# Tail steps carried into the next stream, a root on 128x2, norms tile by tile

## What is computed

```python
for i in range(2):
    mod = (cs @ ada_w[i] + ada_b[i])[:, None, :]          # cs = silu(c)
    sh1, sc1, g1, sh2, sc2, g2 = jnp.split(mod, 6, axis=-1)
    h = rms_norm(x, norm1_g[i]) * (1.0 + sc1) + sh1
    mix = dilated_attention(h, ...) if i == 0 else s5_mixer(h, ...)
    x = x + g1 * mix
    h = rms_norm(x, norm2_g[i]) * (1.0 + sc2) + sh2
    x = x + g2 * conv_ffn(h, ...)       # up product, conv, silu(gate) * up, down product
return rms_norm(x, final_norm_g)        # rms_norm: x * rsqrt(mean(x * x) + 1e-6) * g
```

## Times and profile before

| | us |
|---|---|
| median of 3 runs | 3445.22 (3442.17 to 3446.24) |
| profiled execution | 3444.99 |
| its span, first to last instruction | 3443.2 |
| PE busy | 3022.7 (88% of the span) |
| DVE busy | 2394.6 (70%) |
| ACT busy | 1246.4 (36%) |
| POOL busy | 924.3 (27%) |

### The profile page before, as it was taken

The page is one execution under the profiler, slowest core; times in us unless marked ns, Lnnn a source line. Parts: engine busy times, 40 slices in busy tenths (PEclk is TensorE's granted clock), DMA queues, the critical chain, the costliest instruction groups (busy, mean ns, idle before and its releaser), DMA issues.

```text
span 3443.2 us, 60362 instructions
## 1 busy us (share of the span) xinstructions
PE 3022.7 (88%) x22810; PEld 2833.7 (82%) x22810; DVE 2394.6 (70%) x2649; ACT 1246.4 (36%) x1716; POOL 924.3 (27%) x728
## 2 busy tenths in 40 slices
PE   7899999999769998899988576666997998999997
PEld 3499999999769998899987544443996998999997
DVE  7566666666668887878768698999556664456545
ACT  0144444444224443244432222222433553344432
POOL 2101111111571104720049554555312110001111
PEclk9999999999889999999999797887998999999999
DMA  8977777777556877877667322221553554655453
GB/s 284 340 276 254 258 253 254 253 260 268 190 183 246 301 268 294 301 291 279 240 230 273 137 81 90 79 84 41 180 201 117 183 182 146 186 179 183 165 162 110
DMA packets 227200, 714.37 MB, mean 207 GB/s; under 512 B 40928, under 2 KB 45792, under 8 KB 226656
## 3 DMA queue, kind: packets, MB, share of 16 engines
q1 hardware_dynamic: 185184, 666.98, 56.2%
q10 hardware_dynamic: 41856, 45.19, 4.0%
HBM read 689.01 MB, written 23.07 MB: 207 GB/s over the span
## 4 chain that ended last, share of the span: by engine, by line
PE 67%; DVE 12%; POOL 11%; issue 7%; DMA 2%; ACT 1%; ACTq 0%; DVEq 0%; POOLq 0%
PE proj L1343 21%; PE proj L1344 20%; PE proj L1345 20%; POOL work L1228 3%; POOL work L1224 3%; DVE work L1104 3%; POOL work L1223 2%; DVE raw L1095 2%; DVE work L1098 2%; DVE w_lo L810 1%; DMA ada<-in_ada_w 1%; PE ps L1388 1%; POOL sumsq L1162 1%; DVE work L776 1%; POOL square L1160 1%
## 5 line engine op out<-in xcount | busy, mean ns | idle before, releaser
L810 DVE TENSOR_TENSOR w_lo<-raw,w_hi 128x1024 fp32r<-128x1024 f32 (+1 forms) x896 | 1161.4, 1301 | 761.3 <-ACT w_hi L420 755.7
L1343 PE MATMUL proj<-h_hi,w_hi 128*128 128x256 f32 x5120 | 1482.2, 290 | 180.7 <-POOL h_lo L1168 67.4
L1344 PE MATMUL proj<-h_lo,w_hi 128*128 128x256 f32 x5120 | 1471.5, 287 | 0.0
L1345 PE MATMUL proj<-h_hi,w_lo 128*128 128x256 f32 x5120 | 1470.5, 287 | 0.0
L420 ACT ACTIVATE w_hi<-raw 128x1024 fp32r<-128x1024 f32 (+1 forms) x896 | 925.5, 1043 | 1465.4 <-PE proj L1345 1150.1
L1343 PEld LDWEIGHTS proj<-h_hi,w_hi 128*128 128x128 f32 x5120 | 1006.7, 197 | 198.1 <-issue 174.0
L1344 PEld LDWEIGHTS proj<-h_lo,w_hi 128*128 128x128 f32 x5120 | 1007.4, 197 | 0.0
L1345 PEld LDWEIGHTS proj<-h_hi,w_lo 128*128 128x128 f32 x5120 | 1006.3, 197 | 0.0
L1343 PE MATMUL proj<-a_hi,w_hi 128*128 128x256 f32 x1920 | 562.9, 293 | 85.4 <-DVE x L1005 50.7
L1344 PE MATMUL proj<-a_lo,w_hi 128*128 128x256 f32 x1920 | 557.2, 290 | 0.0
L1345 PE MATMUL proj<-a_hi,w_lo 128*128 128x256 f32 x1920 | 556.9, 290 | 0.0
(11 more groups left out here) (189 smaller groups left out, 2279.7 us busy)
## 6 DMA issues: line engine op xcount, KB each, us to landing
ada<-in_ada_w SPq DMA_DIRECT2D x384, 512.0 KB, 4.7
raw<-in_w_up SPq DMA_DIRECT2D x352, 512.0 KB, 4.3
raw<-in_w_in SPq DMA_DIRECT2D x224, 512.0 KB, 4.7
raw<-in_w_down SPq DMA_DIRECT2D x128, 448.0 KB, 4.5
raw<-in_w_down SPq DMA_DIRECT2D x64, 512.0 KB, 4.4
raw<-in_w_out SPq DMA_DIRECT2D x32, 512.0 KB, 4.3
tab_d<-work ACTq DMA_DIRECT2D x64, 256.0 KB, 4.3
raw<-in_ssm_w_in SPq DMA_DIRECT2D x32, 512.0 KB, 3.8
```

Of the source, the lines that this page charges most:

```text
L810: V.tensor_tensor(w_lo[:, j % LAG, 0:nk * P], raw[:, j % s.ring, 0:nk * P], w_hi[:, j % LAG, 0:nk * P].bitcast(F32), ALU.subtract).then_in ...
L1343: mm(o, w_hi[:, j % LAG, w], hi[:, k, :], start=(k == 0), stop=False)
L1344: mm(o, w_hi[:, j % LAG, w], lo[:, k, :], start=False, stop=False)
L1345: ins = mm(o, w_lo[:, j % LAG, w], hi[:, k, :], start=False, stop=last and k == k0 + nk - 1)
```

## The change

**Carrying.** `run_steps` gets `carry` and `keep`. With `keep`, the steps past the end aren't run in a row but returned, and the next stream takes them as `carry` and runs each after its first steps at the place where the next round would have had it; `sooner(carry, 4)` moves those due later up to step 4. This holds for ACT and DVE at all joints of the feed-forward parts and from gate to ssm_out, and into `split_first` from attn_out, down0b and ssm_out; for POOL at up, up_end and down joints and from gate. The joints qkv to attn_out and ssm_in to gate stay. LO_FIRST is 3.

**Norm.** PE forms the mean with the sum as the stationary operand, so it lands as 128x2 (tokens on partitions, two halves); root, reciprocal and Newton step are 128x2. PE then spreads the result to all partitions by two products of a broadcast column with the identity (`spread_root`). Each tile is one DVE operation (x by scale by root, read from PSUM), one ACT operation (plus shift, to h_hi) and one DVE operation (plus shift, less h_hi, to h_lo), with eight buffers `hf`. POOL has no part in it any more. ACT loads the root's table with a one-column root (`primer`) before it waits for the mean. In the last norm each tile is one DVE operation into a buffer for all 16, and SP's four output DMAs have no buffer to wait for.

**PE's order.** PE waits for h_lo (or a_lo) tile by tile in the first block of a stream. With `cross`, the second and third piece of qkv, of ssm_in and of up0a and up1a change places: piece 2 is the first half of the second block.

**The start.** Norm 0's root is taken in the midst of DVE's factor work (after its 130th step), ACT takes it before the store of ef, and the store of c_new now comes after ACT's part of norm 0. DVE makes the first eight tiles when half of the modulation is there, the others at its end. PE waits for `mod_ready` in place of `norm_link`, since its last ada products now use the first bank again. SP no longer waits for cw_out ahead of the weights. `load_taps(1)` comes before the last gate steps.

```diff
-HI_FIRST, LO_FIRST = 4, 2
+HI_FIRST, LO_FIRST = 4, 3
...
-            if not first:
+            if first:
+                for f in carry.get(j, ()):
+                    f()
+            else:
                 for f in late.get(j + length, ()):
                     f(i - 1)
             for f in late.get(j, ()):
...
-    for due in sorted(late):
-        if due >= length:
-            for f in late[due]:
-                f(count - 1)
+    over = {due - length: [functools.partial(f, count - 1) for f in late[due]] for due in sorted(late) if due >= length}
+    if keep:
+        return over
+    for due in over:
+        for f in over[due]:
+            f()
+    return {}
+def sooner(carry, due):
+    moved = {}
+    for d in sorted(carry):
+        moved.setdefault(min(d, due), []).extend(carry[d])
+    return moved
...
-            def split_first(name):
+            def split_first(name, over):
 
                 for j in range(HI_FIRST):
                     high(st[name])(0, j)
+                    for f in over.pop(j, ()):
+                        f()
+                for due in sorted(over):
+                    for f in over[due]:
+                        f()
...
+            def take_root(number):
+                nc.scalar.activation(primer[:], ones[:, 0:1], ACT.Sqrt)
+                act.wait_ge(norm_link, 5 * number + 1)
+                nc.scalar.activation(root, meansq, ACT.Sqrt).then_inc(root_ready, 1)
+            def norm(number, layer, shift):
+                if number:
+                    take_root(number)
+                for k in range(KT):
+                    act.wait_ge(norm_full, KT * number + k + 1)
+                    nc.scalar.activation(h_hi[:, k, :], hf[:, k % 8, :], ACT.Identity,
+                                         bias=mod[:, layer, shift + k:shift + k + 1], scale=1.0).then_inc(norm_hi, 1)
...
+            take_root(0)
             act.wait_ge(prep_done, 1)
             act.dma_start(ef_d.rearrange("t p n -> p t n"), ef.rearrange("p t a b -> p t (a b)")).then_inc(ef_out, 16)
+            norm(0, 0, 0)
             act.dma_start(cw_d, c_new.rearrange("p t a b -> p t (a b)")).then_inc(cw_out, 16)
-            norm(0)
-            act.wait_ge(norm_lo, 4)
+            act.wait_ge(norm_lo, KT)
             act.wait_ge(cw_out, 16)
             act.dma_start(rel, a["rel"]).then_inc(rel_in, 16)
...
-                    up(f"up{layer}{h}", layer)
-                    up(f"up{layer}{h}_end", layer)
-                    plain(f"down{layer}{h}")
+                    carry = up(f"up{layer}{h}", layer, carry)
+                    carry = up(f"up{layer}{h}_end", layer, carry)
+                    carry = plain(f"down{layer}{h}", sooner(carry, 4), keep=(h == "a" or layer == 0))
+                return carry
...
+            split_first("up0a", plain("attn_out", keep=True))
+            norm(1, 0, 3 * KT)
+            split_first("ssm_in", ffn(0))
+            norm(2, 1, 0)
...
-            act.wait_ge(gg_lo, KT)
+            act.wait_ge(ypre_done, KT)
             load_taps(1)
-            plain("ssm_out")
-            split_first("up1a")
-            norm(3)
+            carry = run_steps(act, s.count, s.length, high(s), late, keep=True)
+            split_first("up1a", plain("ssm_out", sooner(carry, 4), keep=True))
+            norm(3, 1, 3 * KT)
             ffn(1)
-            root(4)
+            take_root(4)
...
+                if links[0] == ROOT_AT:
+                    inverse_root(0)
                 dve.wait_ge(prep_link, links[0])
...
+                base = 5 * number
                 dve.wait_ge(mean_ready, number + 1)
-                V.tensor_scalar(meansq, norm_ps, EPS, None, ALU.add).then_inc(norm_link, 1)
+                V.tensor_scalar(meansq, mean_ps, EPS, None, ALU.add).then_inc(norm_link, 1)
                 dve.wait_ge(root_ready, number + 1)
-                V.reciprocal(rstd[:], rstd[:]).then_inc(norm_link, 1)
-                dve.wait_ge(norm_link, 9 * number + 2)
-                V.tensor_tensor(newton, rstd[:], rstd[:], ALU.mult).then_inc(norm_link, 1)
-                dve.wait_ge(norm_link, 9 * number + 3)
+                V.reciprocal(rstd, root).then_inc(norm_link, 1)
+                dve.wait_ge(norm_link, base + 2)
...
+            def tiles(number, mod_layer, shift, k0, nk):
+                dve.wait_ge(rstd_out, number + 1)
+                def low_part(k):
+                    dve.wait_ge(norm_hi, KT * number + k + 1)
+                    V.scalar_tensor_tensor(out=h_lo[:, k, :], in0=hf[:, k % 8, :],
+                                           scalar=mod[:, mod_layer, shift + k:shift + k + 1],
+                                           in1=h_hi[:, k, :].bitcast(F32), op0=ALU.add, op1=ALU.subtract).then_inc(norm_lo, 1)
+                for k in range(k0, k0 + nk):
+                    if k >= 8:
+                        dve.wait_ge(norm_lo, KT * number + k - 7)
+                    V.scalar_tensor_tensor(out=hf[:, k % 8, :], in0=x[:, k, :], scalar=hscale[:, k:k + 1], in1=rstd_ps,
+                                           op0=ALU.mult, op1=ALU.mult).then_inc(norm_full, 1)
+                    if k >= k0 + 2:
+                        low_part(k - 2)
+                low_part(k0 + nk - 2)
+                low_part(k0 + nk - 1)
...
-            root_mean(0)
-            take_first(0)
-            for q in range(2):
-                by_rstd(0, q, 0)
-            take_first(1)
-            first_scale(0)
-            for q in range(2):
-                by_scale(0, q, 0, 0)
-            for q in range(2, 4):
-                by_rstd(0, q, 0)
-            take_first(2)
-            take_first(3)
-            first_scale(1)
-            for q in range(2, 4):
-                by_scale(0, q, 0, 0)
+            for half in range(2):
+                take_first(2 * half)
+                take_first(2 * half + 1)
+                first_scale(half)
+                tiles(0, 0, 0, 8 * half, 8)
...
+                if shift is not None:
+                    tiles(number, mod_layer, shift, 0, KT)
+                    return
+                dve.wait_ge(rstd_out, number + 1)
+                for k in range(KT):
+                    V.scalar_tensor_tensor(out=normed[:, k, :], in0=x[:, k, :], scalar=hscale[:, k:k + 1], in1=rstd_ps,
+                                           op0=ALU.mult, op1=ALU.mult).then_inc(out_ready, 1)
...
+                    first = isinstance(i, int) and i == 0 and b == 0
                     if k0 == 0:
                         wait(pe, block_out, s.block(i, b) - 1)
                     pe.wait_ge(lo_ready, n + 1)
-                    if isinstance(i, int):
-                        ready(k0 + nk)
                     o = proj[b % 2][:, 0:T]
                     for k in range(k0, k0 + nk):
+                        if first:
+                            ready(k + 1)
...
-                    ins.then_inc(piece_done, 1)
+                    if signals:
+                        ins.then_inc(piece_done, signals)
+                def f(i, j):
+                    if cross and isinstance(i, int) and i == 0 and j in (1, 2):
+                        piece(i, 3 - j, 2 * (j - 1))
+                    else:
+                        piece(i, j, 1)
...
+            def mean(number):
+                pe.wait_ge(sumsq_made, KT * (number + 1))
+                for b in range(2):
+                    ins = mm(mean_ps[:, b:b + 1], sumsq[:, b * P:(b + 1) * P], mean_w[:, 0:1], start=True, stop=True)
+                ins.then_inc(mean_ready, 1)
+            def spread_root(number):
+                pe.wait_ge(norm_link, 5 * (number + 1))
+                for b in range(2):
+                    ins = mm(rstd_ps[:, b * P:(b + 1) * P], rstd[:, b:b + 1].broadcast_to([P, P]), ident[:],
+                             start=True, stop=True)
+                ins.then_inc(rstd_out, 1)
             def norm(number):
-                pe.wait_ge(sumsq_made, KT * (number + 1))
-                mm(norm_ps, mean_w[:], sumsq[:], start=True, stop=True).then_inc(mean_ready, 1)
+                mean(number)
+                spread_root(number)
...
+                    mean(0)
+                if n == 2 * KT + 8:
+                    spread_root(0)
                 if n == 3 * KT:
-                    pe.wait_ge(norm_link, 1)
+                    pe.wait_ge(mod_ready, 1)
```

166 lines of the change are left out of this document (67 added, 99 removed).

## The result

The changed kernel takes 3323.2 us (median of 4 runs, 3322.78 to 3324.42); beside it the kernel before took 3443.7. The ratio is 0.9653, 95% interval 0.9637 to 0.967: 3.5% faster. Forecast were 3331 us and a range of 3310 to 3353. The profiled execution took 3322.78 us, its span is 3320.8, 122.4 less than before.

The account below looks back on a forecast made before the run. PE is busy in most slices, so only its standing still could be won. Norms 46.9, joints 68 and end 4.9, less 5.5 at the start, make 114.3 us: 3445.0 to 3331 us, range 3310 to 3353.

Parts of the forecast that it names:

- Rivals 3, 4 and 5: 3: cw_d store takes 32.6 us, 3357 (0.05); 4: carrying gains nothing, 3399 (0.04); 5: DVE tile operations stretched, 3600 (0.02).
- rivals 1 and 2: 1: POOL's tables eat joint gains, 3352 (0.15); 2: PE's clock stays at 1.00 more, DVE catches up in up0a_end, 3310 (0.13).
- The step from S to the fourth piece: Norms 1 to 3, from the last sum of squares (S) to PE's fourth piece: end at S+22, 16.5 us earlier each.
- POOL's squares: Before norms 1 and 2, slowed by DVE's carried splits: 5 and 2.6 us lost; before norm 3, 1.75 us earlier.
- The table-less joints: Seven joints between streams without POOL table work: idle gaps of 31.7 us plus clock, less 0.5, 45 us won.
- The clock term: PE's slower granted clock (0.50) after a stop at a joint: 2.0 us on the mean, 7 x 2.0 at seven joints.
- down0a and down0b at POOL's pace: Joints into these two streams, paced by POOL's tables and their first factor loads: 4 us won each, not 6.9.
- up0b: Joint into up0b: 7.53 + 2.0, less 1.5 as the last table store holds the first tap; 8 us won.
- The start: Before qkv: the cw_d store lands in 7 us and delays in_rel's load, 5.5 us lost on PE's path.
- The end: Last norm, mean to last tile: 9.4 us instead of 14.6, less 0.3 for the outputs, 4.9 us won.
- Edits at nothing: Small edits expected to cost nothing, among them the primer's 1.28 us table load; uncovered it would cost 1.3 per norm.

Follow-up runs that it names:

- e1_no_carry: The changed kernel with the steps left over at a stream's end run at once, not carried into the next stream; 3391.4 us against 3323.2.
- e10_deep_tables: The changed kernel with in_rel's load behind qkv's fifth split, deeper buffers around POOL's tables and ACT's table stores two steps later; 3308.4 us against 3323.2.
- e9_sooner_up0b: The changed kernel with DVE's steps carried into the up streams due at 2 at the latest instead of 3; 3320.7 us against 3323.2.
- e2_rel_in_qkv: The changed kernel with ACT's wait for the cw_d store and in_rel's load moved behind qkv's fifth split; 3317.8 us against 3323.2.
- e6_no_primer: The changed kernel without the one-column square root that ACT runs before waiting for the mean; 3324.5 us against 3323.2.
- e7_early_qkv: The changed kernel with in_rel's load behind qkv's fifth split and qkv's first weights split before norm 0's last eight tiles; 3318.5 us against 3323.2.

## Why the prediction was right, and where its terms were not

The forecast was 8 us too slow, the sum 114.3 for 122.4. Rivals 3, 4 and 5 fell, rivals 1 and 2 came in part. The mechanisms held at the norms, at the joints without tables, at the end and at the start. At the joints beside POOL's tables they did not: there two terms were off by 7 and 5 us in opposite directions, and that they nearly cancelled is luck.

1. **The step from S to the fourth piece** was right in its rows. In norms 1 and 2: mean 1.0 (1.0 forecast), root steps 1.2 (1.3), spread 1.2 (1.1), first tile S+3.6 (3.5), first h_lo S+5.3 (5.1), last S+16.3 (16.5). In norm 3 the mean took 0.6, and all that follows is 0.5 sooner. A tile comes every 0.79 (0.78). The fourth piece ended at S+20.6, 20.7 and 20.1, and I had taken 22 of 20.5 to 24.5. The mis-sized term is the clock: products were at full pace again (0.28 instead of 0.42) from S+8.9, S+11.2 and S+9.0 on, before the first piece had ended, and not only after the second. Together the three norms gave 59.5 from S on for 54, and the streams behind them took back 3.5 for 1.3. PE's waits for h_lo are 6.3 us, where I had expected a third of 67.4.
2. **POOL's squares** cost 4.4 and 2.8 us (5 and 2.6) and came 1.8 earlier in norm 3 (1.75). "0.7 us of POOL per us of DVE work" held as an estimate. What I did not see is that without carrying the same price is paid on DVE's side, which comes late to the root (e1_no_carry); of that the sum had only the 4.5.
3. **The table-less joints** gave 47.4 (45). The clock term was 1.1 to 2.8 and not 2.0; the gaps were as read. The tightest one, down's third piece, held: PE has no gap at six of the seven, and 0.54 us at ssm_out, for which I had charged 0.5. up0a_end has one gap of 1.6 us, against my sign of under 1.
4. **down0a and down0b at POOL's pace** was the step that failed. The factors were loaded 6.6 us after PE's end (6.4 forecast), so the row was right and the inference wrong: it does not follow that the stream ends only 4 us earlier, since carried tables need not be made by its end. They gave 7.3 and 7.8 for 4 each; that this is the reason is argued, no run takes these two joints apart. POOL's lag of 9.1 us behind PE went into the next stream.
5. **up0b** was the other: 2.6 instead of 8. Counted from the stream's first product, its sixth piece ends at 24.40 us in the changed kernel and at 18.38 in e10_deep_tables, where neither of the two causes below is left: 6.0 lost, for a forecast 1.5. I had priced only the last table's store in front of the first tap; e9_sooner_up0b, where that store is nearly alone, ends the sixth piece at 22.74, so it costs some 4. In front of it stands a term that I had not written down at all: DVE, with ada pieces and splits at 2.1 us, is late with the residual that frees the bank. My check of the tightest joint used unstretched durations (0.48, 0.42) and not the joints beside POOL, where DVE's splits and ada pieces ahead of them are stretched. down0a and up0b together gave 9.9 for a forecast 12.
6. **The start**: cw_d landed after 8.5 us, forecast 7 by the nearest row, inside 2.6 to 32.6; it was issued at 147.31 and not at 149, so 158.60 stood as forecast at 158.5. That the two agree to 0.1 is chance: in the eight kernels whose start is the same qkv's first product comes at 156.7 to 159.9. e2_rel_in_qkv shows that the wait was on PE's path (7.2 us at once), and that not all of it arrives at the end.
7. **The end**: 5.3 (4.9), each tile 0.40. By the Trainium skill, "VectorE: DVE Perf Modes", section "The TRN2 errata — SBUF-src ops pay a fixed extra latency per instruction", cited in the prediction, many small tiles pay a latency each. The trace agrees in part: one operation takes 0.48 and the next starts 0.40 later, so 0.08 of it overlaps, as the forecast had it. Some is still paid: by an estimate from the rows (the same kind of operation takes 0.48 for 256 columns and 1.28 for 1024 in an ada piece, so 0.27 for the 256 columns and 0.21 fixed) 0.13 us of it per tile remains.
8. **Edits at nothing.** The primer is worth nothing, covered or not (e6_no_primer); the 1.3 us that I named for an uncovered load were the wrong mechanism. POOL was 16 us less busy and not 42: the norms took 42.7 off it, and stretching beside carried DVE work put back 16.5 in the tables and 8.8 in the a_lo copies.

Rival 1 (the tables eat the joints) named the right neighbour: up0b lost 5.4 of its 8, but the two down0 joints lost nothing. Of rival 2 the clock in the norms came, 4.6 of its 6 us, the rest did not. Rival 5 has no trace: no tile operation was stretched in a norm.

## What to carry to other kernels

Carrying a stream's tail into the next was worth the gap plus 1 to 3 us of clock here, and where a slower engine's work is carried too, its lag moves with it: find the first step of the next stream that stands behind that work. When two engines slow each other, price both alone and add the two up per window; if the sum is above the window, deeper buffers alone only move the wait (53 us of it vanished from ACT in down0a and the stream was as long as before), and what wins is to move an operation to where it is shorter. That gave 15 us with the old buffers and 33 on top of the deeper ones: the two belong together. Read where a shorter wait comes back before trusting a term: two misses of 5 and 7 us hid in a total that was 8 off.

## What of the hardware was new here

- ACT's function table loads ahead of the wait of the activation that needs it (1.28 us at 2537.32, root held until 2539.06).
- RECIPROCAL on DVE takes 1.75 us at 128x256 where the root's other steps take 0.42, and 0.17 at 128x2.
- Of the 83.7 us that POOL's tables cost in their three streams, PE's idle time makes up 56. Some 21 more are the lower clock: PE was busy for 45.7 us at 0.50 in the three, 2.9 without the tables, and half of such time is lost. The last 6 are restarts: 34 stops, each of which costs the 0.16 us by which one product otherwise overlaps the next.
- The 1 MB store of c_new took 32.6 us right behind the 3 MB store of ef, 8.5 beside the first weight loads, and 14.3 in e7_early_qkv, where it was issued at 99.3.
- A DVE operation that reads one operand from PSUM (0.47 us) keeps its length beside POOL's tables, while a split goes from 1.13 to 1.83.
